# A product-key expert stage whose tokens are spread two at a time by 64-row products, with inner products behind each search and key scores made head by head

## The reference, cut to what matters

```python
q  = (x @ w_q).reshape(S, 8, 2, 128)
s1 = einsum('shd,hnd->shn', q[..., 0, :], k1)        # 8 heads x 128 keys
s2 = einsum('shd,hnd->shn', q[..., 1, :], k2)
v1, i1 = top_k(s1, 16);  v2, i2 = top_k(s2, 16)
cand_s = v1[..., :, None] + v2[..., None, :]         # 256 candidates a head
cand_i = i1[..., :, None] * 128 + i2[..., None, :]
top_s, pos = top_k(cand_s, 16)
experts = take_along_axis(cand_i, pos);  gates = softmax(top_s)
# 128 experts a token (8 heads x 16) of 16384
act = gelu(einsum('ced,cd->ce', u_tab[experts], x)) * gates
out = einsum('ce,ced->cd', act, v_tab[experts])
```

## Time and profile before

| what | us |
|---|---|
| median of 3 runs | 1939.52 (1938.49 to 1941.21) |
| the profiled execution | 1947.71 |
| its span in the profile | 1946.0 |
| PE busy over the span | 1806.9 (93%) |
| DVE busy over the span | 926.9 (48%) |
| HBM read | 617.63 MB, 318 GB/s |

### The profile page before, as it was taken

How to read it: one execution, slowest core, us unless ns; L and a number is a source line. 1 busy time by engine, 2 the same in 40 slices (tenths; PEclk the granted TensorE clock), 3 DMA queues, 4 the chain that set the end, 5 groups by cost and what they waited for, 6 DMA issues and landing times. The chain is left out here.

```text
span 1946.0 us, 23689 instructions
## 1 busy us (share of the span) xinstructions
PE 1806.9 (93%) x9356; PEld 1190.3 (61%) x9356; DVE 926.9 (48%) x1988; ACT 432.9 (22%) x839; POOL 427.8 (22%) x312
## 2 busy tenths in 40 slices
PE   4989999988999999998899999979699999999998
PEld 4975444437787744442675548978588885444443
DVE  4467311123567731112798625966666662222222
ACT  5462111114345321111511424200100110000001
POOL 6820000015668400000300015112022121112110
PEclk7999899998999989999999999999899999999999
DMA  9886799994568589999432333699789999999996
GB/s 394 347 320 217 316 430 429 429 430 170 198 235 313 227 328 430 430 429 429 154 108 87 141 122 118 217 367 389 292 354 391 410 393 373 416 415 403 417 414 269
DMA packets 95089, 620.29 MB, mean 319 GB/s; under 512 B 11520, under 2 KB 12032, under 8 KB 60672
## 3 DMA queue, kind: packets, MB, share of 16 engines
q1 hardware_dynamic: 75824, 482.88, 62.5%
q0 software_dynamic: 18432, 134.23, 17.0%
q10 hardware_dynamic: 720, 1.61, 0.2%
HBM read 617.63 MB, written 1.05 MB: 318 GB/s over the span
## 5 line engine op out<-in xcount | busy, mean ns | idle before, releaser
L3038 PEld LDWEIGHTS bank<-peer_xT,peer_tiles_a 128*128 128x128 f32 x1376 | 160.3, 192 | 21.1 <-issue 12.5
L3038 PE MATMUL bank<-peer_xT,peer_tiles_a 128*128 128x128 f32 x1376 | 164.5, 276 | 6.7 <-DMA peer_tiles_a<-in_peer_u 4.6
L3087 PE MATMUL bank<-peer_tiles_a,peer_H 128*128 128x512 f32 x344 | 159.6, 602 | 6.2 <-DMA peer_tiles_a<-in_peer_v 4.2
L227 POOL TENSOR_TENSOR w_lo<-ring,w_hi 128x1024 fp32r<-128x1024 f32 x60 | 148.3, 2474 | 64.0 <-ACT w_hi L217 63.6
L3262 DVE CUSTOM_DVE_ANT_0 peer_junk<-peer_rows_b,bank 128x1024 bf16<-128x1024 f32 x64 | 78.1, 1220 | 166.8 <-issue 163.8
L1091 PE MATMUL bank<-ring,moe_slots 128*64 128x512 f32 x576 | 132.0, 609 | 9.7 <-DMA ring<-in_stream 9.7
L3058 PE MATMUL bank<-peer_x_rows_hi,peer_ident 128*128 128x512 f32 x256 | 130.6, 510 | 0.4 <-DVE peer_pre L3262 0.3
L3262 DVE CUSTOM_DVE_ANT_0 peer_junk<-peer_rows_a,bank 128x1024 bf16<-128x1024 f32 x48 | 58.6, 1220 | 123.6 <-issue 119.9
L3087 PEld LDWEIGHTS bank<-peer_tiles_a,peer_H 128*128 128x128 f32 x344 | 64.5, 191 | 82.6 <-issue 72.1
L3134 POOL DMA_INDIRECT peer_rows_a<-in_peer_uv,peer_index x48 | 45.5, 949 | 306.5 <-PE bank L3068 263.4
L3134 POOL DMA_INDIRECT peer_rows_b<-in_peer_uv,peer_index x64 | 60.3, 943 | 231.2 <-PE bank L3068 216.3
(11 more groups left out here) (518 smaller groups left out, 3591.6 us busy)
## 6 DMA issues: line engine op xcount, KB each, us to landing
ring<-in_stream SPq DMA_DIRECT2D x103, 2048.0 KB, 12.7
early<-in_stream SPq DMA_DIRECT2D x32, 2048.0 KB, 18.2
peer_tiles_a<-in_peer_u SPq DMA_DIRECT2D x86, 512.0 KB
peer_tiles_a<-in_peer_v SPq DMA_DIRECT2D x86, 512.0 KB
sb_mod_ring<-in_ada_t SPq DMA_DIRECT2D x64, 512.0 KB, 6.3
peer_tiles_b<-in_peer_u SPq DMA_DIRECT2D x42, 512.0 KB
peer_tiles_b<-in_peer_v SPq DMA_DIRECT2D x42, 512.0 KB
ret_mod_ring<-in_ada_t SPq DMA_DIRECT2D x32, 512.0 KB, 5.2
```

The lines of the kernel that those rows point to most:

```text
L227: pool.tensor_tensor(self.shaped(self.w_lo, q, by_columns), self.quarter(n, q, by_columns), self.shaped(self.w_hi, q, by_columns).bitcast( ...
L3038: last = pe.matmul(K.bank[:, 2 + n // 4 % 2, n % 4 * P:(n % 4 + 1) * P], u[:, k, :], xT[:, k, :], start=(k == 0), stop=(k == KD - 1))
L3087: last = pe.matmul(K.bank[:, 2 + dh, :], H[:, m, :], first.slot(n)[:, dh * 512:(dh + 1) * 512], start=(m == 0), stop=(m == PK - 1))
```

## The change

- Key table: it is fetched by one transfer, first thing on SP, into room that is free by then (`K.hT`), and no longer through the ring.
- Key scores: made head by head (two half-heads, both tiles) one quarter after the head's query; ACT takes queries and scores head by head; banks are chosen by `SCORE_BANKS`.
- Spreading: `spread_pair` makes two tokens at once. The stationary and moving operands are partitions 0 to 63 for one token (banks 4, 5) and 64 to 127 for the other (banks 6, 7), eight products of 64 rows in alternation. The order of the tokens (`strip`) puts one of each half into a pair.
- Since pairs now use banks 6 and 7 too, a pair, the gate units and the copies of the choices take turns in them: new waits for `dotted`, `h_gated` and `selT_made`.
- Order: 16 key tiles ahead of the first choices instead of 20; a pair every third tile from tile 24 to 51; DVE takes two dots behind every second search; ACT's exponential of tile 0 stands behind the gelu of tile 63 instead of 59; the groups are worked in rounds of eight key tiles, four gate units and three pairs.

The diff, cut to its core (the GpSimd wait `s_made` goes from 8 to 16, the vector wait before the second picks `s_taken` from 8 to 16):

```diff
-FIRST_TILES = 20
+FIRST_TILES = 16
+SCORE_BANKS = (4, 6, 2, 0)
-TOKENS_FROM = 24
-PICKED_AT = 59
+FIRST_TOKEN = 23
+PICKED_AT = 63
-BESIDE_PICKS = (EARLY - TOKENS_FROM) // 2
+BESIDE_PICKS = 20
+PAIR_AT = {FIRST_TOKEN + 1 + 3 * p: p for p in range(BESIDE_PICKS // 2)}
...
-            fetch_chunks(sp, K, CHUNKS)
+            sp.dma_start(key_rows, K.A["stream"][ROW[n_keys], :, 0:SHORT[n_keys]]).then_inc(keys_in, 16)
...
             for j in range(4):
                 for q in range(Q):
                     query_quarter(j, q)
-                    if j and q == 1:
-                        key_scores(j - 1)
-            key_scores(3)
-            pe.wait_ge(s_taken, 4)
+                    if q == 2:
+                        key_scores(2 * j)
+                    if j and q == 0:
+                        key_scores(2 * j - 1)
+            key_scores(7)
+            pe.wait_ge(s_taken, 12)
...
-            def spread_token(i):
-                if BESIDE_PICKS <= i <= VALUES_FROM + 1:
-                    pe.wait_ge(dotted, i)
-                elif i >= 2:
-                    pe.wait_ge(dotted, i - 1)
-                elif i == 1:
+            def spread_pair(p):
+                if p:
+                    pe.wait_ge(dotted, 2 * p)
+                else:
                     pe.wait_ge(index_made, 1)
-                one = first.ident[:, token(i):token(i) + 1].to_broadcast([P, P])
                 for dh in range(2):
                     for n, part in enumerate(first.x_rows):
-                        last = pe.matmul(K.bank[:, 4 + 2 * buffer_of(i) + dh, :], one, part[:, dh * 512:(dh + 1) * 512], start=(n == 0),
-                                         stop=(n == 1))
+                        for r in range(2):
+                            t, own = token(2 * p + r), slice(64 * r, 64 * (r + 1))
+                            last = pe.matmul(K.bank[:, 4 + 2 * r + dh, :], first.ident[own, t:t + 1].to_broadcast([64, P]),
+                                             part[own, dh * 512:(dh + 1) * 512], start=(n == 0), stop=(n == 1))
                 last.then_inc(spread, 1)
-                if i % QUAD == 1 and i > QUAD:
-                    values_of(i // QUAD - 1)
+
+            def weigh_pair(p):
+                if p % 2 == 0 and p:
+                    values_of(p // 2 - 1)
...
             def gate_unit(m):
                 pe.wait_ge(a_ready, m + 1)
                 pe.wait_ge(b_ready, m + 1)
+                pe.wait_ge(dotted, BESIDE_PICKS + 2 * (3 * (m // 4) + m % 4 // 2 + 1))
...
             turn_picks(0, 6)
+            pe.wait_ge(selT_made, 1)
+            for e in range(GROUPS_LEFT // 2):
+                n, m, p = EARLY + 8 * e, 4 * e, BESIDE_PICKS // 2 + 3 * e
+                spread_pair(p)
                 keys(n)
+                weigh_pair(p)
                 keys(n + 1)
+                gate_unit(m)
+                gate_unit(m + 1)
                 keys(n + 2)
+                pe.wait_ge(h_gated, m + 2)
+                spread_pair(p + 1)
                 keys(n + 3)
+                weigh_pair(p + 1)
+                keys(n + 4)
+                gate_unit(m + 2)
+                gate_unit(m + 3)
+                keys(n + 5)
+                pe.wait_ge(h_gated, m + 4)
+                spread_pair(p + 2)
+                keys(n + 6)
+                weigh_pair(p + 2)
+                keys(n + 7)
...
+            def dot_at(place):
+                i = place + BESIDE_PICKS - 3 * PK_HEADS
+                if i > 0 and i % 2:
+                    dot(i - 1)
+                    dot(i)
...
+            for e in range(GROUPS_LEFT // 2):
+                m, i = 4 * e, BESIDE_PICKS + 6 * e
+                for two in range(2):
+                    dot(i + 2 * two)
+                    dot(i + 2 * two + 1)
+                    if two or e:
+                        gate_tiles(2 * e + two - 1)
+                    gate_h(m + 2 * two)
+                    gate_h(m + 2 * two + 1)
+                    for ahead in range(m + 2 * two + 2, min(m + 2 * two + 4, UNITS)):
+                        gated_hot(ahead)
+                dot(i + 4)
+                dot(i + 5)
```

More of the change, by code:

```diff
@@ L2998, in query_quarter @@
                 query = K.bank[:, 2 * j + q // 2, (q % 2) * T:(q % 2 + 1) * T]
+                if j >= 2 and q == 0:
+                    pe.wait_ge(s_taken, 4 * (j - 1))
                 for k in range(KD):
@@ L3006, in query_quarter, with key_scores @@
                     pe.sem_inc(K.chunk_used, 1)
[L3008 to L3012, removed]
+            def key_scores(h):
+                if h == 0:
+                    pe.wait_ge(keys_in, 16)
+                keys = key_rows.rearrange("p (m n) -> p m n", n=PK)
+                pe.wait_ge(q_taken, h + 1)
                 for n, tt in enumerate((1, 0)):
[L3014 to L3017, removed]
+                    for m in (2 * h, 2 * h + 1):
+                        last = pe.matmul(K.bank[:, SCORE_BANKS[h // 2] + n, m % 4 * PK:(m % 4 + 1) * PK], qT[:, m, tt * P:(tt + 1) * P],
+                                         keys[:, m, :], start=True, stop=True)
                     last.then_inc(s_made, 1)
@@ L3198, in _ @@
                     exponential(0)
-                if n % 2 == 1 and n > TOKENS_FROM:
-                    spread_walked((n - TOKENS_FROM) // 2)
-            for g in range(GROUPS_LEFT):
-                i = BESIDE_PICKS + 3 * g
-                spread_walked(i)
-                spread_walked(i + 1)
-                gelu(EARLY // 4 + g)
-                spread_walked(i + 2)
-            for i in range(VALUES_FROM, TOKENS):
-                spread_walked(i)
+                if n in PAIR_AT:
+                    pair_walked(PAIR_AT[n])
+            for e in range(GROUPS_LEFT // 2):
+                p = BESIDE_PICKS // 2 + 3 * e
+                pair_walked(p)
+                gelu(EARLY // 4 + 2 * e)
+                pair_walked(p + 1)
+                pair_walked(p + 2)
+                gelu(EARLY // 4 + 2 * e + 1)
+            for p in range(VALUES_FROM // 2, TOKENS // 2):
+                pair_walked(p)
             act.activation(warm[:], eps[:], ACT.Sqrt)
@@ L3232, in pick_head @@
                 c.settle()
+                dots_at(3 * h + 2)
             def recover(tt):
@@ L3304, in _ @@
             dve.sem_inc(index_made, 1)
-            dve.wait_ge(s_taken, 8)
+            dve.wait_ge(s_taken, 16)
             for h in range(PK_HEADS):
-                pick_head(0, h)
-                for i in range(max(h - 1, 0) * BESIDE_PICKS // (PK_HEADS - 1), h * BESIDE_PICKS // (PK_HEADS - 1)):
-                    dot(i)
+                pick_head(0, h, dot_at)
             recover(0)
@@ L3318, in _ @@
             dve.wait_ge(gelu_done, EARLY // 4)
-            for g in range(GROUPS_LEFT):
-                m, i = 2 * g, BESIDE_PICKS + 3 * g
-                dot(i)
-                if m < UNITS:
-                    gate_h(m)
-                if m + 2 < UNITS:
-                    gated_hot(m + 2)
-                dot(i + 1)
-                if m + 1 < UNITS:
-                    gate_h(m + 1)
-                if m + 3 < UNITS:
-                    gated_hot(m + 3)
-                dot(i + 2)
-                gate_tiles(g)
+            for e in range(GROUPS_LEFT // 2):
+                m, i = 4 * e, BESIDE_PICKS + 6 * e
[10 more added lines that the diff above has]
+                dot(i + 5)
+            gate_tiles(GROUPS_LEFT - 1)
             for i in range(VALUES_FROM, TOKENS):
```

87 lines of the change are left out of this document (41 added, 46 removed).

## The result

The kernel after takes **1924.5 us** (median; 1922.1 to 1926.1), the kernel before, run beside it, 1940.4 (1938.5 to 1945.2). The ratio is 0.9916, 95% interval 0.9897 to 0.9934: 0.84% or 16 us faster. The forecast was 1916.5, with a range of 1903 to 1936. The profiled execution took 1925.9 us, its span 1924.1. Two kernels of the experiments had one execution each far out of line (2190.7 and 10120.7 us), which medians and ratios leave out.

What follows compares the result with a forecast made beforehand. From the first gather on, bytes and what leaves the DMA queue short were taken as the bound. -16.5 up to the second turning and -7 in the groups, taken as -23, gave 1925 profiled, 1916.5 median; range 1903 to 1936.

Steps and rivals of the forecast that it cites:

- The bound and the direction: From the first gather on, bytes and what leaves the DMA queue short of them set the time; faster, 87%.
- Key table and scores: Front of the stage: DVE starts its searches 9 us earlier and the first gather moves 7 us earlier, -7.
- The 2 us charged for more collisions on DVE: Searches at the front: more heads fall beside POOL's work and slow DVE's casts, 2 us (0 to 4).
- 16 tiles instead of 20: Ahead of the first gather: four key tiles fewer in hand, 2.1 MB, +5; PE waits some 4 us there.
- The second turning: PE turns tile 0's choices at 1385 instead of 1401.75 us; with the front and 16 tiles, -16.5 together.
- The pair: Spreading two tokens with both halves at once takes 1.1 us, switches of shape included (to 2.0).
- The groups: Rounds of eight key tiles: PE falls to 24.0 us, DMA takes over at 25.4; -7 (-12 to +14).
- The 5 us allowed for the start: Groups: allowance for four gathers waiting for the first `values_of` and for rows that come late.
- serial halves: Rival: a pair's halves run one after the other or the switch drains; pair 2.0 us, total 1923; 13%.
- bare handoffs: Rival: in the groups gate handoffs stay uncovered, two a round at 2.5 us; total 1938, no change; 10%.
- The value tiles: Last stretch, already full at 413 GB/s: halved spreading only adds idle time, 0 (to -3).
- the hole stays: Rival: dots wait for late gathers, choices come at 1395, low DMA before the second turning remains; total 1926; 9%.

Runs made afterwards that it cites:

- early exponential: Kernel after with ACT's exponential of tile 0 back behind the gelu of tile 59 instead of 63: 1915.4 us, ratio 0.9871.
- whole rows: Kernel after with each token of a pair spread by products of all 128 rows again, order kept: 1931.3 us, ratio 0.9954.
- after again: Kernel after once more, unchanged, for a second profile: 1922.5 us, ratio 0.9911 to the kernel before.
- Half-size tiles: Kernel after fetching only 512 of 1024 columns of each value tile, PE's work unchanged, output incomplete: 1896.1 us, ratio 0.9771.
- table alone: Kernel before with only the key table fetched at once in one transfer, scores at their old place: 1941.6 us, ratio 0.9999.
- table and scores: Kernel before with the key table fetched at once and scores made head by head, nothing else changed: 1940.7 us, ratio 1.0002.
- before again: Kernel before once more, unchanged, for a second profile: 1943.1 us, ratio 0.9995.

## Why the prediction was right, and what of it was off

**The bound and the direction: right.** Over the kernels that take the whole work, the stage's length goes with the lost time: 771 us at 42.2, 758 at 30.3, 749 (mean of two) at 21.4, 743 at 15.9. That is 28 us of stage for 26 of queue. This alone proves little, since all of them move the same bytes: a shorter stage must show less lost time. It says where the time went. That bytes bind is shown by an experiment only for the value tiles; for the searches PE's waits for key tiles say so, and in the groups PE still paces, with the bytes just behind it.

**Key table and scores: sizes close, credit wrong.** The first search came at 10.3 behind Q (forecast 10.5), the first gather 10.5 us earlier instead of 7. The 2 us charged for more collisions on DVE had the wrong sign: the casts lost 6.9 us to POOL before and lose 1.3 now. The earlier trace rows show one of 2.11 us, but the dearest took 3.64, and it was there to be read. Alone the part is worth nothing in the time.

**16 tiles instead of 20: the wait was not there.** I had PE wait some 4 us at the first turning. It waits for nothing, as the choices are ready at 1254.94 and PE ends its 16 tiles at 1258.2. With 20 tiles the gather comes 7 us later and the time is the same within the intervals, so what the four tiles cost and what the earlier gather gives about cancel.

**The second turning: the step that failed by itself.** I had PE through tile 63 at 1380.5, 205.5 behind Q, and the turning at 1385. PE was through at 212.4 and the turning came at 215.8, so this part gave 10.9 us instead of 16.5. My 1380.5 carried over the stage's old bytes. Both kernels issue 24 gathers ahead of the turning, but the last four were issued from 200.7 to 204.4 behind Q before, 5 to 9 us ahead of PE's end there, so that part of their bytes moved in the hole. Now all are issued by 1359.99, 186.1 behind Q, and stand ahead of the last key tiles: four gathers are 4.2 MB, an estimated 10 us of queue at 413 GB/s. PE waits for tiles 17.4 us in all from the first turning to tile 63, where it waited 4.9, and when the gathers have landed nothing is left to move but the tiles (297, then 74 GB/s). The last step, PE's end to turning, was right: 3.35 us against 3.5. I charged no more for it than its length; the early exponential shows that it cost 7 to 9, together with the slow clock behind it.

**The pair: right.** 1.12 us against 1.1. Its switch is seen in full only one step later, 0.19 us on the next tile. Together 1.3 us against 1.85 for whole rows. By the Trainium skill (TensorEngine Tiling (Array Packing), Key Properties) a change of tiling mode drains TensorE. The rows agree that there is a cost of changing shape (0.2 us in 1.12 against 0.92, and 0.19 behind it), and the whole-rows kernel shows that it stays below the gain.

**The groups: larger than forecast.** Rounds of 24.9 us instead of 25.4, and 204.7 us from the second turning to the first value tile instead of 217.3: -12.6 against -7. The 5 us allowed for the start was not needed, as the 40 us behind the turning run at 396 GB/s. The whole-rows kernel gives the cause: 26.5 a round on PE without the halves, and 216.3 us for the same stretch. I had PE at 24.0 a round, with the bytes taking over at 25.4. PE's round is 24.9, mostly because more of its eight tiles stand behind a change of shape (15.2 us of them instead of 14.3), and the bytes do not take over before the end. The rivals of serial halves and bare handoffs fall with it: products go in twos, and PE has no wait in the chain.

**The value tiles: 0 was nearly right.** From the first value tile to the end it is 329.8 and 326.6 us, after and after again, against 327.0 and 327.5 before. Half-size tiles show the bound.

**The sum, and the term that set the miss.** At the second turning 10.9 and in the groups 12.6 make 23.5, the sum that I had. That is luck: the first is 5.6 below its share and the second 5.6 above. The value tiles of this execution gave 2.8 back, and its Q lies 1.2 earlier, which has nothing to do with the change; so the span fell by 21.9 against 23, and the profiled time was forecast as 1925 and was 1925.9. The median, forecast as 1916.5, was 1924.5. In number it lies nearer to two rivals, 1923 (serial halves) and 1926 (the hole stays), than to the forecast, and only the marks rule these out. Of the signs named beforehand, the wait at the second turning (3.35 us, under 6) came true; the first gather (1259.75 instead of 1263 to 1266) and the rounds (24.9 instead of 25 to 26) came out better, the second turning (1389.64 instead of 1382 to 1388) worse, and no sign of being wrong showed.

What was off is the last step, "the profiled execution is 8.2 us above the median of the runs": I took 8.2 off the forecast too, as if that distance belonged to the kernel. It does not. The profile of after stands 1.4 above its median and that of after again 2.4 below; the second profile of before is 2.5 above its own, and those of table alone and of table and scores, kernels that take the same time as before, are 2.8 and 4.4 below theirs, with stages of 766 to 767 us and not 771 to 773. Some 4 of the 8.2 us lie ahead of the stage (Q at 1175.05 against 1170.84 in before again), the rest in it. Over the four profiles of kernels that take the time of before, the stage is 769 us long on average, and 749 over the two of after: 20 us less, where the medians say 16 to 17.5. So part of the gain that I read from one execution was never there. Why one execution is several us longer than another is open.

## What to carry to other kernels

Where bytes and compute are close, cost an edit by the queue time that it saves or loses, window by window: a start 3 us earlier gave nothing, while a wait of 3.35 us, with the slow clock behind it and the later gathers, cost 7 to 9. An experiment has to tell what such queue time is worth, since lost time and length go together in any case. When long work is moved ahead of a meeting point, look at what else (here one exponential on another engine) still stands behind the last tile. And take the baseline of a forecast from more than one profiled execution, or from one near the median, before subtracting a difference of terms from it.

## What the runs showed of the hardware

- Products of 64 rows on the two halves of the array run at once (0.39 us for two and 1.12 for eight, against 0.62 and 1.85 with 128 rows), and the tile behind a change of shape takes 0.19 us more.
- Through PE's 3.35 us without work ahead of the turning the granted clock reads 1.00; in the 3.4 us behind it, with PE at work again, it reads 0.64, so most of that stretch is at the 1.2 GHz level, and the same products take 0.63 instead of 0.39 us. With the wait gone it is 1.00, the 2.4 GHz level, throughout. The Trainium skill (TensorE: Matmul & The Clock Gate, Part 1) has the clock follow how busy TensorE was; the traces agree. Here the fall comes behind the idle time; in the kernel before, where PE waits 17.14 us, it comes inside the wait: the clock reads 1.00 from 1386 to 1387 and 0.50 from 1388 to 1389, with PE idle in both.
- A queue of 0.5 MB tiles and 1 MB gathers moves 410 to 416 GB/s over the full stretches of 158 and 280 us.
- A cast of 32 numbers on DVE takes 0.18 us when POOL is not at work and up to 3.64 us beside POOL's filling of H.
